# Router reordered in a one-core trunk layer: expert columns gathered directly, slots broadcast by a product, third ring quarter freed early

## What is computed

```python
x = ln_affine(alpha * x + g1 * mix, ln1_g, ln1_b)      # mix = merged @ w_out
h = ln_plain(x) * (1 + sc2) + sh2
x = ln_affine(alpha * x + g2 * moe(h), ln2_g, ln2_b)

def ec_moe(h, w_router, w_gate, w_up, w_down):          # context and latent apart
    aff = softmax(h @ w_router)                         # 16 experts
    gate, idx = top_k(aff.T, cap)                       # cap = 16 context, 32 latent
    xe = take(h, idx)
    hid = silu(xe @ w_gate[e]) * (xe @ w_up[e])         # 1024 -> 2816
    ye = (hid @ w_down[e]) * gate
    out[idx] += ye
```

## Time and profile before

| what | value |
|---|---|
| median of 3 runs | 1865.33 us (1864.21 to 1867.61) |
| the profiled execution | 1867.64 us, of it 1865.8 us span |
| mean granted TensorE clock | 0.972 of full |
| PE busy | 1672.9 us (90%) |
| DVE, ACT, POOL busy | 503.0, 338.3, 46.3 us |
| moved by DMA | 642.04 MB, mean 344 GB/s over the span |

### The profile page before, as it was taken

The page is one execution under the profiler, slowest core; times in us unless marked ns, Lnnn a source line. Parts: engine busy times, 40 slices in busy tenths (PEclk is TensorE's granted clock), DMA queues, the critical chain, the costliest instruction groups (busy, mean ns, idle before and its releaser), DMA issues.

```text
span 1865.8 us, 18738 instructions
## 1 busy us (share of the span) xinstructions
PE 1672.9 (90%) x7753; PEld 799.4 (43%) x7753; DVE 503.0 (27%) x956; ACT 338.3 (18%) x663; POOL 46.3 (2%) x71
## 2 busy tenths in 40 slices
PE   5999999999977998998988999798998989999896
PEld 2767787778763333333333323233333323333232
DVE  5385547775672101011010101101011010101102
ACT  2443355553321000000000000000000000000000
POOL 2001000010010000000000000000000000000000
PEclk9999999999988999999999999999999999999998
DMA  9683343325559999999999999999999999999994
GB/s 355 219 278 98 110 125 90 91 76 182 188 201 376 431 431 429 432 428 431 433 429 430 431 430 430 431 433 428 428 433 429 431 431 431 429 431 429 431 432 184
DMA packets 60569, 642.04 MB, mean 344 GB/s; under 512 B 6142, under 2 KB 6286, under 8 KB 32878
## 3 DMA queue, kind: packets, MB, share of 16 engines
q1 hardware_dynamic: 56464, 629.96, 81.6%
q0 software_dynamic: 4064, 11.54, 1.9%
HBM read 637.77 MB, written 3.71 MB: 344 GB/s over the span
## 4 chain that ended last, share of the span: by engine, by line
PE 67%; DMA 22%; DVE 7%; ACT 2%; issue 2%; POOL 0%; SPq 0%; DVEq 0%; ACTq 0%; POOLq 0%
PE banks L1038 24%; DMA ring<-in_w_exp_down 16%; PE banks L740 15%; PE banks L1060 11%; PE banks L1068 4%; DMA ring<-in_w_exp_up 4%; PE banks L1021 2%; PE banks L738 2%; PE banks L696 1%; PE banks L755 1%; DMA ring<-in_w_in 1%; PE banks L896 1%; DVE O L1786 1%; PE banks L1026 1%; DMA O<-in_ln_b 1%
## 5 line engine op out<-in xcount | busy, mean ns | idle before, releaser
L1038 PE MATMUL banks<-ring,O 128*64 128x512 f32 (+1 forms) x3072 | 641.5, 576 | 27.6 <-DMA ring<-in_w_exp_up 13.8
L1038 PEld LDWEIGHTS banks<-ring,O 128*64 128x64 f32 x3072 | 219.6, 134 | 441.3 <-issue 414.3
L1060 PE MATMUL banks<-ring,O 128*64 128x512 f32 x1408 | 328.3, 623 | 25.1 <-DMA ring<-in_w_exp_down 15.0
L1060 PEld LDWEIGHTS banks<-ring,O 128*64 128x64 f32 x1408 | 101.6, 144 | 242.0 <-issue 195.3
L1781 DVE TENSOR_TENSOR O<-O,banks 128x512 f32<-128x512 f32 (+1 forms) x48 | 28.0, 639 | 650.3 <-PE banks L1038 650.3
L740 PE MATMUL banks<-slot_parts,X_parts 128*128 128x512 f32 x672 | 183.4, 403 | 0.0
L740 PEld LDWEIGHTS banks<-slot_parts,X_parts 128*128 128x128 f32 x672 | 121.3, 188 | 39.5 <-issue 11.0
L1786 DVE TENSOR_TENSOR O<-banks,O 128x512 f32<-128x512 f32 x32 | 20.6, 687 | 390.1 <-PE banks L1060 390.1
L740 PE MATMUL banks<-slot_parts,H_parts 128*128 128x512 f32 x432 | 115.7, 396 | 0.4 <-DVE X L1397 0.4
L1463 DVE TENSOR_TENSOR slot_parts<-ring,slot_parts 128x512 fp32r<-128x512 f32 x176 | 110.2, 687 | 16.6 <-ACT slot_parts L1107 15.8
L1068 PE MATMUL banks<-O 128*128 128x512 f32 x192 | 86.6, 601 | 22.4 <-DVE O L1786 22.4
(11 more groups left out here) (252 smaller groups left out, 1070.7 us busy)
## 6 DMA issues: line engine op xcount, KB each, us to landing
ring<-in_w_exp_gate SPq DMA_DIRECT2D x64, 2816.0 KB, 30.6
ring<-in_w_exp_up SPq DMA_DIRECT2D x64, 2816.0 KB, 26.1
ring<-in_w_exp_down SPq DMA_DIRECT2D x32, 3072.0 KB, 23.5
ring<-in_w_exp_down SPq DMA_DIRECT2D x16, 4096.0 KB, 28.0
ring<-in_w_in SPq DMA_DIRECT2D x16, 2048.0 KB, 9.9
ring<-in_w_mod SPq DMA_DIRECT2D x16, 1024.0 KB, 10.8
ring<-in_w_exp_down SPq DMA_DIRECT2D x16, 1024.0 KB, 32.3
O<-in_w_mod SPq DMA_DIRECT2D x8, 1024.0 KB, 5.3
```

Of the source, the lines that this page charges most:

```text
L1038: x = pe.matmul(banks[64 * w:64 * w + 64, 3 * m + b, 0:(i1 - i0) * P], xeT[:, k % 4, 64 * (k // 4):64 * (k // 4) + 64], w4[:, kk, w, i0 * ...
L1060: x = pe.matmul(banks[64 * w:64 * w + 64, 6 + dc, :], hidT[:, i, 64 * w:64 * w + 64], wd[:, i, w, dc * BANK:(dc + 1) * BANK], start=(i == ...
```

## The change

1. Ring: the wait for the last output job moves from quarter 2 to quarter 3. `mT_low` moves out of the ring into `O4_parts`, laid out by tile.
2. `merged_low(0)` and `merged_low(1)` are issued inside the loop over `J_PB` instead of behind it.
3. Norms of tiles 1 and 2: VectorE computes only -mean/deviation (`nmr`, one column); ScalarE makes x * rstd + nmr in one step; POOL multiplies by the scale and adds the shift, in halves of 512 columns (four instructions a tile instead of one).
4. Order: PE runs `J_WO[5]` before it turns h2; VectorE copies jobs 4 and 5 with half of the statistics between them and no softmax; h2 of tile 0 is made, turned and used in halves; the maximum is taken negated in one instruction.
5. Top-k works on the turned probabilities where they lie in PSUM. Latent rounds have the softmax of tile 0 in between; the latents' slots are broadcast while the context's rounds run.
6. The first expert's selection is made by a product that broadcasts its slots over all partitions and compares them with the row number. Ten products without use (`keep_busy`) stand before and between.
7. Every expert's columns are gathered directly: h2's channels are the stationary operand, the selection (32 columns) is the moving one, 24 products in place of 6 products and 4 transposes. ScalarE and VectorE each copy half of the result.
8. `slot_bc` is made by 16 products between gate and up of the first expert, which stands outside the loop; the way through HBM is gone. POOL's loads of the last norm's rows wait for it (`rt_all`).

```diff
-        mT_high, mT_low = cols(H_r[:]), oaT_low
+        mT_high, mT_low = cols(H_r[:]), O4_r[:].rearrange("p (t k n) -> p k t n", t=T, n=P)
...
+        h2_cols = O4[:].rearrange("p (t n k) -> p t k n", t=T, k=KT)
+        xeT = O3[:, BANK:2 * BANK].rearrange("p (k s) -> p k s", k=KT)
...
             for q in range(4):
-                if q == 2:
+                if q == 3:
                     wait_job_copied(sp, J_WO[-1])
...
                 pool.wait_ge(h2_norm, n + 1)
-                pool.tensor_tensor(h2[:, t, :], h2[:, t, :], sh2b[:, min(t, 1), :], ALU.add).then_inc(h2_ready[n], 1)
+                for w in range(2):
+                    cs = slice(w * BANK, (w + 1) * BANK)
+                    pool.tensor_tensor(h2[:, t, cs], h2[:, t, cs], sc2b[:, g, cs], ALU.mult).then_inc(h2_scaled, 1)
+                    pool.wait_ge(h2_scaled, 2 * n + w + 1)
+                    pool.tensor_tensor(h2[:, t, cs], h2[:, t, cs], sh2b[:, g, cs], ALU.add).then_inc(h2_ready[n], 1)
...
-            pool.wait_ge(rt_slots, 1)
-            pool.dma_start(slot_tokens, slots[:, 0:SLOT]).then_inc(rt_stored, 16)
-            pool.wait_ge(rt_stored, 16)
-            pool.dma_start(slot_bc, slot_tokens.rearrange("e s -> (e s)")[None].to_broadcast((P, NE * SLOT))).then_inc(rt_bc, 16)
-            pool.wait_ge(rt_tt, 1)
+            pool.wait_ge(rt_all, 1)
             pool.dma_start(l2g, ln2_g.to_broadcast((P, D))).then_inc(ld_end, 16)
             pool.dma_start(l2b, ln2_b.to_broadcast((P, D))).then_inc(ld_end, 16)
...
+            wait_job_copied(pe, J_WO[-1])
+            keep_busy(8)
...
+            def gather(k, ts):
+                s0 = k % 4 * SLOT + (LAT0 if ts[0] else CTX0)
+                for t in ts:
+                    x = pe.matmul(banks[:, 6 + k // 4, s0:s0 + CAP_L], h2_cols[:, t, k, :], sel[:, t, :],
+                                  start=(t == ts[0]), stop=(t == ts[-1]))
+                return x
+            pe.wait_ge(rt_lat, 1)
+            pe.matmul(banks[:, 1, 0:CAP_L], one_expert(0), slots[:, 0:CAP_L], start=True, stop=True).then_inc(rt_first, 1)
+            pe.wait_ge(sel_ready, 2)
+            for k in range(KT):
+                gather(k, (1, 2))
+            keep_busy(2)
+            pe.wait_ge(rt_ctx, 1)
+            pe.matmul(banks[:, 1, CAP_L:SLOT], one_expert(0), slots[:, CAP_L:SLOT], start=True, stop=True).then_inc(rt_first, 1)
+            pe.wait_ge(sel_ready, 3)
+            for k in range(KT):
+                x = gather(k, (0,))
...
-                pe.wait_ge(sel_ready, e * T + T)
+                if not first:
+                    pe.wait_ge(sel_ready, e * T + T)
+                    for k in range(KT):
+                        gather(k, (1, 2))
+                        x = gather(k, (0,))
+                    x.then_inc(xet_done, 1)
+                pe.wait_ge(xet_cp, 2 * e + 2)
                 pe.wait_ge(acc_done, e * 6 + 6)
-                for t in range(T):
-                    for w in range(2):
-                        x = pe.matmul(banks[64 * w:64 * w + 64, 3, :], sel[:, t, :], h2_half(t, w),
-                                      start=(t == 0), stop=(t == T - 1))
-                x.then_inc(xe_done, 1)
-                pe.wait_ge(xe_cp, e + 1)
-                for i in range(4):
-                    x = pe.transpose(banks[:, 4, i * P:(i + 1) * P], xe_cols[:, i, :], ident)
...
+                    if first and m == 0:
+                        broadcast_slots()
+                        pe.wait_ge(rt_cols, 2)
...
+                act.activation(h2[:, t, :], x_r[:, t, :], ACT.Identity, scale=s("rstd", t, t + 1),
+                               bias=s("nmr", t, t + 1)).then_inc(h2_norm, 1)
```

More of the change, by code:

```diff
@@ L972, in turn_probs, with keep_busy @@
                 pe.wait_ge(rt_aff, n + 1)
-                pe.transpose(banks[0:NE, 4 + t, 0:P], aff[:, t, :], ident).then_inc(rt_tr, 1)
+                pe.transpose(lat_probs[:, (t - 1) * P:t * P] if t else context_probs, aff[:, t, :], ident).then_inc(rt_tr, 1)
+            def keep_busy(n):
+                for _ in range(n):
+                    pe.matmul(banks[:, 0, 0:256], ident, kf[:, 0:256], start=True, stop=True)
             wait_tile(pe, F_M, 0)
@@ L984, in _ @@
             job(J_WO[4])
-            pe.wait_ge(h2_ready[0], 1)
+            job(J_WO[5])
+            pe.wait_ge(h2_ready[0], 2)
             turn_tile(h2, 0)
-            job(J_WO[5])
-            logits(0)
-            pe.wait_ge(h2_ready[1], 1)
-            turn_tile(h2, 1)
-            turn_probs(0)
-            logits(1)
-            pe.wait_ge(h2_ready[2], 1)
-            turn_tile(h2, 2)
+            for b in range(2):
+                logits(0, b)
+            for n in (1, 2):
+                for b in range(2):
+                    pe.wait_ge(h2_ready[n], b + 1)
+                    turn_half(h2, n, b)
+                    if n == 2 and b:
+                        turn_probs(0)
+                    logits(n, b)
@@ L1008, in rows_so_far, with broadcast_slots @@
+            pe.transpose(banks[:, 3, NE:2 * NE], gates, ident[0:NE, 0:NE]).then_inc(rt_tt, 1)
+            def broadcast_slots():
+                for e in range(NE):
+                    x = pe.matmul(banks[:, 6 + e // 8, e % 8 * SLOT:(e % 8 + 1) * SLOT], one_expert(e), slots[:, 0:SLOT],
+                                  start=True, stop=True)
+                x.then_inc(rt_all, 1)
             def rows_so_far(ns):
@@ L1069, in expert @@
                                   start=not last, stop=True, skip_group_check=last).then_inc(comb_done, 1)
-            with pe.Fori(0, NE - 1) as e:
+            expert(0, first=True)
+            with pe.Fori(1, NE - 1) as e:
                 expert(e)
@@ L1337, in _ @@
                                    ACT.Copy).then_inc(hidt_cp, 1)
+            expert(0)
+            with act.Fori(1, NE) as e:
+                act.wait_ge(xet_done, e + 1)
+                act.activation(xeT[:, 0:4, :], banks[:, 6, 0:4 * SLOT].rearrange("p (k s) -> p k s", s=SLOT), ACT.Copy).then_inc(xet_cp, 1)
+                expert(e)
             for t in range(T):
@@ L1794, in expert @@
                         dve.tensor_tensor(dst, dst, banks[:, n, :], ALU.add).then_inc(acc_done, 1)
-            with dve.Fori(0, NE - 1) as e:
+            expert(0, first=True)
+            with dve.Fori(1, NE - 1) as e:
                 expert(e)
```

240 lines of the change are left out of this document (130 added, 110 removed).

## The result

| | before | after |
|---|---|---|
| median of 4 runs | 1865.99 us (1864.21 to 1867.61) | 1966.17 us (1963.56 to 1973.79) |
| ratio, 95% interval | | 1.0544 [1.0511, 1.0576] |
| the profiled execution | 1867.64 us | 1968.06 us |
| mean granted TensorE clock | 0.972 | 0.920 |
| first gate product of the experts | 580.88 us | 586.21 us |

Slower by 100 us; the forecast was 1863.9 with a range up to 1872.0. The page of after, in parts: busy time, shares of the chain, three of the costliest groups.

The account below looks back on a forecast made before the run. The DMA's stream of expert loads was taken as the bound, PE having 4.3 us an expert in hand. Terms -4.5 + 2.4 + 0.4 + 0.3 = -1.4 us gave a median of 1863.9, range 1857.0 to 1872.0.

Parts of the forecast that it names:

- Strided weights cost no more in the nearest row: Each expert's gather: 11 transposes with columns 11 apart took 0.146 us each, so 48 records were priced at 0.116 us.
- The term of +0.4 us (bound +1.9): From end of spreading to next gate in each expert: 6.3 us instead of 5.87, under the slack, so counted as nothing.
- the 4.3 in hand: PE's slack per expert in the kernel before: its path takes 76.1 us, the stream of loads 80.4.
- The gather makes the PE the bound: Rival in the experts: clock falls in the 32-column stream, 0.214 us a record; +36 us full size, likelier 1878; chance 0.12.
- my 1.7: In that rival, the us an expert lost because the first gate products behind the gather also run slow.
- Forecast 576.4: Start of the first expert's gate: 576.4 us instead of 580.88, 4.5 earlier; bounds 573.2 and 582.6.
- nobody waits for them: POOL's eight half instructions in the norms replace two of 2.3 us and end near 545 for tile 2, delaying nobody.
- forecast 558.2: First top-k round of latents: 558.2 us instead of 562.30, 4.1 of VectorE's 6.5 us gain left.
- The third quarter at nothing: Ring: loading the third gate quarter (2.88 MB, 6.7 us) early costs and gains nothing, covered by the hole before the restart.
- signs of an error: DMA below 425 GB/s mid-run, gate start outside 573 to 583, or no last-norm loads inside the stream.
- The broadcast product: Between gate and up of the first expert: 32 records hold up the PE 1.7 to 3.7 us, taken as 2.7.
- the rule of the Trainium skill that I quoted: Loading a stationary operand takes as long for few rows as for 128; the broadcast's 16 products would cost 3.7 us.

Follow-up runs that it names:

- the wide products: Seven unused products of 256 columns put between the groups of each looped gather, against the kernel with h2 stored in the gather's order: 1881.62 us, ratio 1.0078 to before.
- the run with the gather of before: The changed kernel with before's gather in every expert and no products without use, first selection still by the broadcast product: 1866.25 us, ratio 1.0005 to before.
- the HBM version: Changed kernel with before's gather, no products without use, last norm's rows loaded early, slots broadcast through HBM again: 1865.87 us, ratio 1.0001 to before; repeated, 1863.42 us.
- the measurement: Kernel before plus streams of 16 products ahead of its first transposes, stationary columns 1 to 16 elements apart; 0.114 us a record at distance 1; total time says nothing.
- the permuted version: The changed kernel with h2 written in the gather's order, so its stationary columns are adjacent, weights' layout in the ring kept: 1890.75 us, ratio 1.0121 to before.

## Why the prediction was wrong

**The step that failed** is "Strided weights cost no more in the nearest row", in the part on each expert. It took 48 records at 0.116 us = 5.55; they measured 11.24 us, 0.234 each. The term of +0.4 us (bound +1.9) is +6.0. The row I took it from the earlier trace rows holds transposes, one record each, where the cost is small in the whole; a product was the thing to compare with, and no row of before has an fp32 product with a stationary operand of such columns. A sign was in the trace all the same: the load of the stationary operand alone took 213 ns there, against 141 for transposes of adjacent columns. Since the operation stood in no row, its upper bound should have been the slowest record of a 128-column load at hand, 0.214 us: 48 x 0.214 = 10.3 us, 4.7 more than the 5.55 that I took and more than the 4.3 in hand. I had that record, and used it only for the rival.

**The rival that came nearest.** "The gather makes the PE the bound" gave 0.214 us a record, 83.0 us an expert on the PE and +36 us at full size. Measured were 0.234, 85.8 and +100, so it was right in kind and short in size. The records cost about what it said, for another reason; the fall of the clock it named came as well, and cost 1.8 us an expert behind the gather against my 1.7. With adjacent columns, where its mechanism is the one that is left, the kernel lost 25 us (1890.75). I gave it 0.12 and weighed it at 1 us an expert on average, because before runs at 1.00. But before has no narrow stream in its experts: its clock said nothing of one. The Trainium skill, TensorE: Matmul & The Clock Gate, section on HAM oscillation, speaks of bursts between waits. Here the PE had no wait at all from 747.5 to 758.75 and fell to half in the middle of it, so the outcome is the rule's and its cause isn't.

**The sum as measured.** From the runs: 75 us for the distance of the columns (1966.17 to 1891.18 or 1890.75), 24 us for the narrow gather and the products without use (1890.75 to 1866.25), of which 9 are the clock in the experts at least (1890.75 to 1881.62), and nothing measurable for the rest of the change. These are differences in this order; with the clock at half before the distance is removed, part of its cost would count as the clock's.

**The start.** Forecast 576.4, measured 586.21. The two parts of the gather took 11.85 us instead of 5.6 (+6.2), the products without use let the broadcast out at 570.2 instead of 568.0 (+2.2), the second pair of them 1.87 instead of 0.9 (+1.0). VectorE lost 1.9 us before the last output job, beside POOL's halves. I had said of these that nobody waits for them, and had not asked whom they slow down. The Trainium skill, GPSIMD Engine Reference, section Specifications, has POOL's way into SBUF shared with VectorE, with contention for VectorE instructions of two SBUF inputs; the two lengthened ones have two, and each took over 0.9 us more, while a BATCH_NORM_STATS2, with one input, took its 1.29 us beside POOL (531.39), so the trace agrees. The first round of the latents came at 560.73 (forecast 558.2). With before's gather and no products without use the first gate was at 576.20, 575.88, 575.62, 575.33 and once 579.18; that this is near my 576.4 is chance, since that sum had 6 us of such products and the narrow gather in it.

**Right.** The DMA as the bound of before with 4.3 us an expert in hand: at 85.8 us on the path (+9.7) the loads fell to 379 GB/s, and at 79.1 (with the wide products) they ran at 430 again. The third quarter at nothing. MAX8 from PSUM took 0.42 us as from SBUF. Two things that I had listed as signs of an error came: 379 GB/s in the middle, and a gate start outside 573 to 583.

**Mis-sized.** The broadcast product took 3.71 us, my upper bound, against 2.7: so the rule of the Trainium skill that I quoted (the load counts columns, not rows) was the better price, and the trace agrees with it. In some versions it has a larger cost that I did not have, the half clock behind it: up took 22.89 us in the run with the gather of before. In the changed kernel itself it stayed at 20.08 us, at full clock.

**Open.** Why a distance of 8 elements costs double at full clock isn't shown, only that it does, and from which distance on isn't either; how the gain of the early start, 5.3 us at the last landing of the loads in the profiled execution of the HBM version (1806.15 against 1811.41), shrinks to 1 to 2 in the median isn't settled beyond the spread of the clock's rise.

## What to carry to other kernels

Price a new instruction by rows of the same kind with the same layout; where there is none, take the slowest of its size as the bound, and if that crosses the slack, the rival has to carry weight. A loop whose engine has 4 us in hand out of 80 stands one doubled term from being bound by it. A stage that looks shorter by columns may be longer by its loads, and it can change the clock of the stage behind it.

## What the runs showed that I had not expected

- An fp32 product with 128 stationary columns takes 0.114 us a record with adjacent columns at full clock and 0.220 at half. At a distance of 8 elements it takes 0.237 to 0.239 at full clock, and 0.234 over the gather of the changed kernel, about half of it at half clock: at full clock the distance costs as much as the half clock does, and at half it adds little.
- A stream of products with 32 moving columns went from a clock of 1.00 to 0.50 with the PE busy throughout (34.4 to 39.8 us of the measurement: 0.63, then 0.50), and 39.9 us of gate and up became 42.2. It does not fall in every such stream: late in the permuted version 48 records ran at full clock nearly to their end. Useless products with 256 columns inside the stream kept it at 1.00 and won 9 us.
- Useless products ahead of the first gather made it shorter but the start later: with contiguous columns 32 records took 7.04 us without them and 5.41 with them, while the products themselves held the PE for 6.5 us. The first gate came 6.3 us later with them, and the medians were the same.
- VectorE instructions of 1024 columns with two inputs in SBUF took 1.66 to 2.20 us beside POOL's halves, 1.28 alone; the two halves beside the first two of them took 2.28 and 2.13 instead of 1.3.
